# Weight blocks split once: pass 2 stores both parts in scratch memory, passes 3 and 4 fetch them

## The chip, the cores and the metric

The kernel runs on one core of a Trainium2 chip. The metric is the time of one execution on the device in microseconds (us), as the median of several runs. The engines are TensorE (PE, with its weight loads PEld), VectorE (DVE), ScalarE (ACT), GpSimd (POOL) and SyncE (SP), which here issues all DMA transfers, in one queue and in program order.

## The reference, cut to what matters

One layer of a decoder: an adaLN-modulated RMS norm, one input projection, a sliding-window attention branch (A) and a gated linear recurrence (B), each projected and merged by sigmoid gates, an output projection, and a gated residual. There are 2048 prompt positions (D_MODEL 1024) and 8 sample positions with caches of their own, all in float32.

```python
h = rms_norm(x, norm_g) * (1 + scale) + shift
proj = h @ w_in                      # qa, ka, va, za, qb, fb, ib, zb
ya = window_attention(qa, k_all, v_all, pos0, sinks) * silu(za)
o, s_new = hgrn2_chunked(qb, log_f, k_in, ib, s0)
yb = rms_norm(o, o_norm_g) * silu(zb)
g_a, g_b = split(sigmoid(h @ w_merge + b_merge), 2)
y = g_a * (ya @ w_proj_a) + g_b * (yb @ w_proj_b)
out = x + gate * (y @ w_out)
```

## The kernel before

The prompt is worked on in four passes (`it` 0 to 3, called pass 1 to 4) of 512 positions. A pass has 68 units of dense matmuls (`UNITS`): four each of B, A, za, f, qb, ib and zb, then 32 merge units (ga, gb, pa, pb), then four each of o0 and o1, the two halves of the output projection. The units alternate between two PSUM banks, D0 and D1. Each unit is done in two halves, and between the halves each engine runs the small tasks that `SIDE` lists for that place: transposes, attention, the recurrence, and in passes 1 and 2 the work for the sample rows.

The weights are 58 blocks (`BLOCKS`) of 128 x 1024 floats, 512 KB each, and every pass reads all of them again. To keep float32 precision, each factor is split into a high part in the matmul's reduced format and the low rest, and a product is three matmuls: high x high, high x low, low x high. A block comes by DMA into one of three raw buffers (`w_raw`). ACT copies it into the high part (`split_hi`, L969), POOL subtracts in four pieces to get the low part (`split_lo`, L1691). Both parts go into one of eight slots (`w_hi`, `w_lo`; `SLOT`), two of which the attention's output holds for part of a pass. `HOLDER[n]` is the unit that reads the slot's former block last, `SPOT[n]` the unit at which block n is split, planned so that the split is some 7 cost units (a unit of 24 matmuls counts 4) ahead of the first use. A unit waits for the semaphore w_lo of its last block.

SP's order is written out: `weights(n)` loads raw block n when block n - 3 is split and, in passes 1 and 2, when the sample rows have been multiplied with it in its raw form (the task `bu`, L807 to L814; two blocks at a time where `PAIR` says so). Other transfers (x tiles, stores of the result, caches, the sample's states) are events with a due unit, put into the same queue ahead of the first weight load that is due later. Among them, at the end of pass 1 and the start of pass 2, are the stores of the result rows, and the eight state loads `s_st` (L616), 256 KB each. POOL scales a state (L1751), DVE adds the product of PE's task `vB` (L1626), and PE uses it in the task `so` (L856).

Before the first pass PE transposes four tiles of x (`x_turn`, L704). Two are done ahead of the first unit, two are tasks inside it (L154, L155).

Of the kernel before, what the change touches and what calls it, by code (L numbers as in the profile page):

```python
# [15 lines left out]
TB, NIT = 512, 4  # L16
# [119 lines left out]
def put(it, u, hf, task, a, bank=None, key=None):  # L136

    SIDE.setdefault((it, u, hf), []).append((task, a, bank, key or (it, task, a)))
# [12 lines left out]
    put(it, n // 2, n % 2, *rest)  # L151


put(0, 0, 0, "xturn", 2)  # L154
put(0, 0, 1, "xturn", 3)  # L155
for it in range(NIT):
    if it == 0:
        put(0, 3, 0, "gm", 0, "XA")
# [88 lines left out]
for _it in range(NIT):  # L247
    for _u in UNITS:
        if _u in TH:
# [6 lines left out]
           "lvl", "dgp", "at0", "smax", "p_exp", "p_norm", "kst", "on", "yf", "yh", "yl", "y7f", "y7h", "y7l", "x_in0", "x_in1", "xst", "rstd",  # L256
           "xn", "xm", "xh0", "xh1", "h_hi", "h_lo", "grow", "s_rows", "s_th", "s_sq8", "s_sc", "s_exp", "s_p", "ckv", "s_oT",
           "s_f", "s_ib", "esel", "s_sq", "s_yb", "s_y", "s_o", "s_o1", "s_win", "s_st_out", "xsr"]
        + ["vr"] + [f"xr{t}" for t in range(NT)] + [f"out{t}" for t in range(NT)] + [f"s_st{b}" for b in range(NS)]
        + [f"ada{k}" for k in range(2 * KT)] + [f"gw{p}" for p in range(4)]  # L260
        + ["p_late", "p_load0", "p_load1", "p_load2", "p_load3", "p_load4", "p_c", "p_T", "p_xs", "p_mod", "hm", "p_vec", "p_lb", "p_exp0", "p_rows", "p_scale", "p_x2",
           "p_x3", "p_bg", "fin", "w_lo0", "act_step", "dve_step", "pool_step"])


def h_pairs(it, n):
# [54 lines left out]
def build(nc, A, O):  # L320

    ctx = ExitStack()
    with ctx:
# [95 lines left out]
        def f32(ap):  # L419
            return ap.bitcast(F32)  # L420
# [34 lines left out]
        XA, XB, XC, XD = (pb[b] for b in ("XA", "XB", "XC", "XD"))  # L455
        S = {n: ctx.enter_context(nc.semaphore("s_" + n)) for n in SEMS}

        def flat(t, n):
            return t.rearrange("p h n -> p (h n)")[:, 0:n]

# [15 lines left out]
            return [(w_raw[:, n % NRAW], A["w_blocks"][n % NB].rearrange("p (k c) -> p k c", k=KT))]  # L476

        came, _c = [], [0] * NRAW
        for n in range(NIT * NB):
            _c[n % NRAW] += 16 * len(block_dmas(n))  # L480
            came.append(_c[n % NRAW])
        bursts, bursts_so_far = {}, 0
# [15 lines left out]
        def _(sp):  # L498
# [21 lines left out]
            for k in range(KT):  # L520
                ada_load(k, 0)

            def weights(n):
                if n >= NRAW:
                    s.wait_ge("w_lo", n - NRAW + 1)
                    if n - NRAW in bursts:
                        s.wait_ge(*bursts[n - NRAW])
                for dst, src in block_dmas(n):
                    load(dst, src, f"w_in{n % NRAW}")
# [116 lines left out]
            load(sink_s[:, :], A["sinks"].rearrange("a h -> h a"), "p_load4", allow_slow_non_contiguous=True)  # L646
            s.full(-1, "xT", 1)
            load(bg, A["b_ada"][:, 2 * D:3 * D].broadcast_to([P, D]), "p_bg")
            for n in range(NRAW, NIT * NB):
                while events and events[0][0] <= max(SPOT[n - NRAW], BURST_AT.get(n - NRAW, 0)):  # L650
                    event(*events.pop(0)[1])
                weights(n)
            for _, e in events:
                event(*e)
            s.wait_ge("k_sc", NIT)
# [12 lines left out]
        def _(pe):  # L668
# [18 lines left out]
            def turn_rows(h):  # L687
                bank, c = ((pb["D0"], 0), (XC, P))[h]
                for i in range(8):
                    n = 4 * h + i % 4 + 8 * (i // 4)  # L690
                    ins = mm(bank[:, c + 9 * i:c + 9 * i + 9], mod_rows[:, P * n:P * n + P], sel, start=True, stop=True)
                s.done(ins, "p_T")
# [21 lines left out]
            ada_half(1)  # L714
            s.wait_ge("p_rows", 4)
            turn_rows(1)

            def dense(it, u, hf_):
                kind, j = UNITS[u]
                blocks = unit_blocks(u)  # L720
                bank = pb[f"D{u % 2}"]
                s0, nb = SLOT[blocks[0]], len(blocks)
                if hf_ == 0:
                    s.wait_ge(f"D{u % 2}_free", (it * NU + u) // 2)
                    s.wait_ge("w_lo", it * NB + blocks[-1] + 1)
                    if (kind, j) == ("pa", 0):
                        s.wait_ge("yl", 16 * it + 4)
                    if (kind, j) == ("pb", 0):
                        s.wait_ge("yl", 16 * it + 8)
                hi, lo, k0, nk = h_hi, h_lo, 0, KT  # L730
                if kind == "pa":
                    hi, lo, nk = ya_hi, ya_lo, 4
                elif kind == "pb":
                    hi, lo, k0, nk = yb_hi, yb_lo, 4, 4
                elif kind in OUT_COLS:
                    hi, lo = y_hi, y_lo
                if it == 0 and u < NT:
                    s.wait_ge("h_lo", (1, 3, 2, 4, 5, 6, 7, 8)[2 * u + hf_])
                for k in range(hf_ * nk // 2, (hf_ + 1) * nk // 2):
                    if it and u == 0:  # L740
                        s.wait_ge("h_lo", h_pairs(it - 1, k // 2))
                    if u == 60:
                        s.wait_ge(*(("yl", 16 * it + 9 + k) if k < 7 else ("y7l", it + 1)))
                    if u == 61:
                        s.wait_ge("yl", 16 * it + 16)
                    for r, (w, a) in enumerate(((w_hi, hi), (w_hi, lo), (w_lo, hi))):
                        go, end = (k == 0 and r == 0), (k == nk - 1 and r == 2)
                        if kind in ("A", "B", "ib", *OUT_COLS):
                            ins = mm(bank[:, 0:P * nb].rearrange("p (n c) -> p n c", c=P), a[:, k, P * j:P * j + P],  # L749
                                     w[:, s0:s0 + nb, k, :], start=go, stop=end)  # L750
                        else:
                            ins = mm(bank[:, :], w[:, s0, k0 + k, :], a[:, k, :], start=go, stop=end)  # L752
                if hf_:
                    s.done(ins, f"D{u % 2}_full")
# [206 lines left out]
        def _(act):  # L961
# [3 lines left out]
            def split_hi(n):  # L965
                s.wait_ge(f"w_in{n % NRAW}", came[n])
                if HOLDER[n] >= 0:
                    s.unit_full(*divmod(HOLDER[n], NU))
                s.done(fn(w_hi[:, SLOT[n % NB]], w_raw[:, n % NRAW], ACT.Copy), "w_hi")  # L969

            def squares(src, t, junk):
# [163 lines left out]
            for it in range(NIT):  # L1135
                for u in range(NU):
                    for hf_ in (0, 1):
                        if hf_:
                            evac(it, u)
                            if UNITS[u] == ("pb", 7):  # L1140
                                s.wait_ge("y7f", it + 1)
                                s.done(fn(y_hi[:, 7, 0:P], yf[:, 1, 0:P], ACT.Copy), "y7h")
                                s.wait_ge("yf", 8 * it + 8)
                                s.done(fn(y_hi[:, 7, P:TB], yf[:, 1, P:TB], ACT.Copy), "yh", 16 * it + 16)
                            for n in ATTACH.get(it * NU + u, []):
                                split_hi(n)
                        for task, a, _, key in SIDE.get((it, u, hf_), []):
                            side(it, task, a, key)
                            if task == "PV":
                                s.freed(it, "PV", a)  # L1150
                                if it == 1 and a == 0:
                                    s.wait_ge("s_st_out", 16 * NS)
                                high(ya_hi[:, :, P * a:P * a + P], 16 * it + a)
                            if task == "PV" and a == 3:
                                s.done(fn(kT[:, 0:P], kT[:, TB:TB + P], ACT.Copy))
                                s.full(it, "PV", 3)
                                s.done(fn(vtok[:, 0, :], vtok[:, NT, :], ACT.Copy))
                            if task == "yT":
                                s.freed(it, "yT", a)
                                high(yb_hi[:, :, P * a:P * a + P], 16 * it + 4 + a)  # L1160
                        if hf_ and UNITS[u][0] == "pb" and UNITS[u][1] < 7:
                            j = UNITS[u][1]
                            s.wait_ge("yf", 8 * it + j + 1)
                            high(y_hi[:, j, :], 16 * it + 8 + j)
# [518 lines left out]
        def _(pool):  # L1683
# [34 lines left out]
            for it in range(NIT):  # L1718
                for u in range(NU):
                    for hf_ in (0, 1):  # L1720
                        if hf_:
                            if UNITS[u] == ("pb", 7):
                                s.wait_ge("y7h", it + 1)
                                s.done(g_.tensor_tensor(y_lo[:, 7, 0:P], yf[:, 1, 0:P], f32(y_hi[:, 7, 0:P]), ALU.subtract), "y7l")
                                s.wait_ge("yh", 16 * it + 16)
                                s.done(g_.tensor_tensor(y_lo[:, 7, P:TB], yf[:, 1, P:TB], f32(y_hi[:, 7, P:TB]),
                                                        ALU.subtract), "yl", 16 * it + 16)
                            for n in ATTACH.get(it * NU + u, []):
                                split_lo(n)
                        for task, a, _, key in SIDE.get((it, u, hf_), []):  # L1730
                            if task == "at0":
                                if it:
# [105 lines left out]
```

## Time and profile before

| | |
|---|---|
| Median of 3 runs | 1563.0 us (1561.78 to 1563.56) |
| The profiled execution | 1561.99 us, its span 1559.9 us |
| Mean granted TensorE clock | 0.998 |
| PE, ACT, DVE, POOL busy | 98%, 35%, 51%, 53% of the span |
| Bytes moved by DMA | 178.94 MB, 115 GB/s on average |

The span runs from the first to the last instruction. Busy times of different engines overlap. A matmul's end is modelled, so a busy PE is not a PE at its peak. The chain of waits follows the work that ended last back to its start. A wait is put down to the instruction that released it. The granted clock is 1.0 at 2.4 GHz and 0.5 at 1.2 GHz.

### The profile page before, as it was taken

Reading aid. Unit: us, or ns where it says so; the run is one execution under the profiler, and the core shown is the slowest. Engines: PE = TensorE matmul, PEld = TensorE weight load, DVE = VectorE, ACT = ScalarE, POOL = GpSimd, SP = SyncE. Lnnn points to the kernel's source line nnn. Section 1 sums busy time; section 2 is a strip of 40 time slices with the busy share of each in tenths; the row PEclk is TensorE's granted clock in tenths of the full one; section 3 lists DMA queues with packets and bytes.
Section 4 is the critical chain, followed back from the end, with each engine's and each line's share of the span. In section 5 each row is a group of like instructions: output and inputs, shape, how many; then the busy total and the mean of one; then the engine's idle time right before and its main releaser. Section 6 shows DMA issues by size and latency. Waiting matters only on the chain.

```text
span 1559.9 us, 31668 instructions
## 1 busy us (share of the span) xinstructions
PE 1529.6 (98%) x13056; PEld 1242.1 (80%) x13056; DVE 792.2 (51%) x1900; ACT 541.2 (35%) x1119; POOL 821.8 (53%) x1074
## 2 busy tenths in 40 slices
PE   5999999999999999999999999999999999999998
PEld 2777778877888778887779878888888877788887
DVE  5767464234578866231544774622453775623132
ACT  4334324344322532434331452243432353143330
POOL 1525434557863643365783472437886363437671
PEclk9999999999999999999999999999999999999999
DMA  9612211334464221233343331223543231222241
GB/s 343 237 55 83 83 57 55 114 130 162 163 197 114 103 69 61 77 109 109 136 175 124 102 110 42 83 70 113 207 155 145 75 109 56 75 72 92 103 167 59
DMA packets 62791, 178.94 MB, mean 115 GB/s; under 512 B 7087, under 2 KB 18696, under 8 KB 61865
## 3 DMA queue, kind: packets, MB, share of 16 engines
q1 hardware_dynamic: 62648, 176.93, 32.4%
q8 instruction: 103, 1.69, 0.4%
q14 instruction: 40, 0.32, 0.1%
HBM read 162.84 MB, written 11.96 MB: 112 GB/s over the span
## 4 chain that ended last, share of the span: by engine, by line
PE 94%; DVE 3%; SPq 1%; DMA 1%; issue 1%; ACT 0%; POOL 0%; DVEq 0%
PE ps_D L752 56%; PE ps_D L749 25%; PE ps_XD L814 2%; PE ps_XA L912 1%; SPq L502 1%; PE ps_XB L890 1%; PE ps_XB L938 1%; PE ps_XA L943 1%; PE ps_XB L937 1%; PE ps_XA L923 1%; PE ps_XA L890 1%; DMA th_t<-in_w_ada 1%; PE ps_XB L923 1%; PE ps_XC L825 0%; PE ps_XC L930 0%
## 5 line engine op out<-in xcount | busy, mean ns | idle before, releaser
L1691 POOL TENSOR_TENSOR w_lo_t<-w_raw,w_hi_t 128x256 fp32r<-128x256 f32 x920 | 677.0, 770 | 604.6 <-ACT w_hi_t L969 604.1
L752 PE MATMUL ps_D<-h_hi_t,w_hi_t 128*128 128x512 f32 x1024 | 412.2, 403 | 0.0
L752 PE MATMUL ps_D<-h_lo_t,w_hi_t 128*128 128x512 f32 x1024 | 399.7, 390 | 0.0
L752 PE MATMUL ps_D<-h_hi_t,w_lo_t 128*128 128x512 f32 x1024 | 399.6, 390 | 0.0
L969 ACT ACTIVATE w_hi_t<-w_raw 128x1024 fp32r<-128x1024 f32 x232 | 240.0, 1051 | 121.7 <-PE ps_D L749 61.6
L752 PEld LDWEIGHTS ps_D<-h_hi_t,w_hi_t 128*128 128x128 f32 x1024 | 192.3, 188 | 47.2 <-issue 10.1
L752 PEld LDWEIGHTS ps_D<-h_hi_t,w_lo_t 128*128 128x128 f32 x1024 | 192.2, 188 | 41.8
L752 PEld LDWEIGHTS ps_D<-h_lo_t,w_hi_t 128*128 128x128 f32 x1024 | 192.5, 188 | 36.2
L749 PE MATMUL ps_D<-w_hi_t,h_hi_t 128*128 128x384 f32 (+1 forms) x384 | 141.7, 369 | 4.1 <-POOL w_lo_t L1691 3.1
L749 PE MATMUL ps_D<-w_hi_t,h_lo_t 128*128 128x384 f32 (+1 forms) x384 | 136.6, 356 | 0.0
L749 PE MATMUL ps_D<-w_lo_t,h_hi_t 128*128 128x384 f32 (+1 forms) x384 | 136.4, 355 | 0.0
L749 PE MATMUL ps_D<-w_hi_t,y_hi_t 128*128 128x512 f32 x256 | 100.2, 391 | 1.5 <-issue 1.5
L749 PE MATMUL ps_D<-w_lo_t,y_hi_t 128*128 128x512 f32 x256 | 99.7, 389 | 0.0
L749 PE MATMUL ps_D<-w_hi_t,y_lo_t 128*128 128x512 f32 x256 | 99.6, 389 | 0.0
L749 PEld LDWEIGHTS ps_D<-w_hi_t,h_hi_t 128*128 128x128 f32 x384 | 72.7, 189 | 15.0 <-issue 4.9
L1365 DVE SCALAR_TENSOR_TENSOR acc_t<-th_t,ps_D 128x512 f32<-128x512 f32 x24 | 16.5, 688 | 130.9 <-PE ps_D L752 130.8
L1036 ACT ACTIVATE th_t<-ps_D,bm_half 128x512 f32<-128x512 f32 x48 | 33.1, 689 | 139.2 <-PE ps_D L752 139.2
L1112 ACT ACTIVATE p_or_hf<-p_or_hf,sm 128x160 f32<-128x160 f32 x128 | 53.4, 419 | 77.5 <-DVE sm L1492 74.3
L749 PEld LDWEIGHTS ps_D<-w_lo_t,h_hi_t 128*128 128x128 f32 x384 | 72.6, 189 | 5.3
L749 PEld LDWEIGHTS ps_D<-w_hi_t,h_lo_t 128*128 128x128 f32 x384 | 72.8, 190 | 4.7
L1445 DVE TENSOR_TENSOR qq<-qq,ff 128x1024 f32<-128x1024 f32 x28 | 40.7, 1452 | 69.3 <-PE ps_XB L890 44.8
L1534 DVE SCALAR_TENSOR_TENSOR state<-state,ff,ps_XA 128x128 f32<-128x128 f32 x64 | 18.0, 342 | 112.4 <-PE ps_XA L943 112.4
(399 smaller groups left out, 2338.3 us busy)
## 6 DMA issues: line engine op xcount, KB each, us to landing
w_raw<-in_w_blocks SPq DMA_DIRECT2D x232, 512.0 KB, 3.3
xr<-in_x_prompt SPq DMA_DIRECT2D x16, 512.0 KB, 5.6
x_or_AT<-in_x_prompt SPq DMA_DIRECT2D x14, 512.0 KB, 4.5
out_dram<-xr SPq DMA_DIRECT2D x12, 512.0 KB, 2.9
x_or_AT<-in_x_turned SPq DMA_DIRECT2D x3, 1024.0 KB, 6.8
p_or_hf<-in_x_turned SPq DMA_DIRECT2D x3, 1024.0 KB, 7.4
out_dram<-xr SPq DMA_DIRECT2D x8, 256.0 KB, 2.0
ibtok<-vtok SPq DMA_DIRECT2D x8, 192.0 KB, 2.9
```

The source lines that it names most:

```text
L749: ins = mm(bank[:, 0:P * nb].rearrange("p (n c) -> p n c", c=P), a[:, k, P * j:P * j + P], w[:, s0:s0 + nb, k, :], start=go, stop=end)
L752: ins = mm(bank[:, :], w[:, s0, k0 + k, :], a[:, k, :], start=go, stop=end)
L814: ins = mm(dst, hS[:, k, :], raw[:, :, k, :], start=k < 4, stop=k >= 4)
L890: ins = mm(bank[row:row + left, m * col:m * col + m], kk[:, h, c + 32 * g:c + 32 * g + left], right, start=True, stop=True)
L923: ins = mm(dst[DH * g:DH * g + DH], val[:, DH * g:DH * g + DH], PT[r, g, :, 32 * j:32 * j + 32], start=j == 0, stop=j == 4)
L969: s.done(fn(w_hi[:, SLOT[n % NB]], w_raw[:, n % NRAW], ACT.Copy), "w_hi")
L1036: s.leave(fn(dst, bank[:, :], ACT.Tanh, scale=0.5, bias=bm_half[:, c:c + 1]), it, u)
L1112: fn(p_t[:, m, :], p_t[:, m, :], ACT.Exp, bias=negm[:, m:m + 1], accum_out=rsum[:, m:m + 1])
L1365: leave(stt(acc[:, :], thx("ga", j), 1.0, bank[:, :], ALU.add, ALU.mult), it, u)
L1445: s.done(tt(qr, qr, fl[:, :, :, 0:1].broadcast_to(shape), ALU.mult))
L1534: ins = stt(state[:, h, :], state[:, h, :], ff[:, h, P * a:P * a + 1], bank[:, P * h:P * h + P], ALU.mult, ALU.add)
L1691: ins = g_.tensor_tensor(w_lo[:, c, k:k + 2], w_raw[:, n % NRAW, k:k + 2], f32(w_hi[:, c, k:k + 2]), ALU.subtract)
```

## The change

In pass 2 the blocks are loaded and split as before, and SP then also stores both parts of each block into a scratch tensor in device memory (`kept`). In passes 3 and 4 raw loads and splits are gone: SP fetches both parts of a block from the scratch tensor straight into the slot, as soon as the slot's former block has been read for the last time. PE waits for the slot's fetches (`w_got`) there instead of for w_lo. A split into a slot waits until the slot's stores have landed (`w_kept`). Apart from that, one transposition of x is moved from inside the first unit to just ahead of it.

```diff
-put(0, 0, 0, "xturn", 2)
-put(0, 0, 1, "xturn", 3)
+put(0, 0, 0, "xturn", 3)
...
+def slot_loads(n):
+
+    return sum(SLOT[m % NB] == SLOT[n % NB] for m in range(2 * NB, n + 1))
+
+
+def slot_stores(n):
+
+    return sum(SLOT[m % NB] == SLOT[n % NB] for m in range(NB, min(n, 2 * NB)))
...
+        kept = nc.dram_tensor("w_kept", [NB, 2, P, KT * P], F32, kind="Internal").ap()
...
-        for n in range(NIT * NB):
+        for n in range(2 * NB):
             _c[n % NRAW] += 16 * len(block_dmas(n))
...
+            def keep(n):
+                if n >= NB:
+                    c = SLOT[n % NB]
+                    for h, w in enumerate((w_hi, w_lo)):
+                        load(kept[n % NB, h], f32(w[:, c]).rearrange("p k c -> p (k c)"), f"w_kept{c}")
+
+            def fetch(n):
+                c = SLOT[n % NB]
+                s.unit_full(*divmod(HOLDER[n], NU))
+                s.wait_ge(f"w_kept{c}", 32 * slot_stores(n))
+                for h, w in enumerate((w_hi, w_lo)):
+                    load(f32(w[:, c]).rearrange("p k c -> p (k c)"), kept[n % NB, h], f"w_got{c}")
+
             def weights(n):
                 if n >= NRAW:
                     s.wait_ge("w_lo", n - NRAW + 1)
+                    keep(n - NRAW)
                     if n - NRAW in bursts:
                         s.wait_ge(*bursts[n - NRAW])
...
-            for n in range(NRAW, NIT * NB):
+            for n in range(NRAW, 2 * NB):
                 while events and events[0][0] <= max(SPOT[n - NRAW], BURST_AT.get(n - NRAW, 0)):
                     event(*events.pop(0)[1])
                 weights(n)
+            for n in range(2 * NB - NRAW, 2 * NB):
+                while events and events[0][0] <= max(SPOT[n], BURST_AT.get(n, 0)):
+                    event(*events.pop(0)[1])
+                s.wait_ge("w_lo", n + 1)
+                keep(n)
+            for n in range(2 * NB, NIT * NB):
+                while events and events[0][0] <= HOLDER[n]:
+                    event(*events.pop(0)[1])
+                fetch(n)
...
+            x_turn(-1, 2, x_p[2])
...
-                    s.wait_ge("w_lo", it * NB + blocks[-1] + 1)
+                    if it < 2:
+                        s.wait_ge("w_lo", it * NB + blocks[-1] + 1)
+                    else:
+                        for b in blocks:
+                            s.wait_ge(f"w_got{SLOT[b]}", 32 * slot_loads(it * NB + b))
...
+                s.wait_ge(f"w_kept{SLOT[n % NB]}", 32 * slot_stores(n))
                 s.done(fn(w_hi[:, SLOT[n % NB]], w_raw[:, n % NRAW], ACT.Copy), "w_hi")
...
                             for n in ATTACH.get(it * NU + u, []):
-                                split_hi(n)
+                                if n < 2 * NB:
+                                    split_hi(n)
...
+                                if it == 2 and a == 0:
+                                    for c in (NSLOT, NSLOT + 1):
+                                        s.wait_ge(f"w_kept{c}", 32)
...
                             for n in ATTACH.get(it * NU + u, []):
-                                split_lo(n)
+                                if n < 2 * NB:
+                                    split_lo(n)
```

## Rows read from the trace of the kernel before

**Rows 1.** The page: engines' busy time, and two costliest groups of the split.

```profile
PE 1529.6 (98%) x13056; PEld 1242.1 (80%) x13056; DVE 792.2 (51%) x1900; ACT 541.2 (35%) x1119; POOL 821.8 (53%) x1074
...
L1691 POOL TENSOR_TENSOR w_lo_t<-w_raw,w_hi_t 128x256 fp32r<-128x256 f32 x920 | 677.0, 770 | 604.6 <-ACT w_hi_t L969 604.1
...
L969 ACT ACTIVATE w_hi_t<-w_raw 128x1024 fp32r<-128x1024 f32 x232 | 240.0, 1051 | 121.7 <-PE ps_D L749 61.6
```

**Rows 2.** Windows: passes 2, 3, 4; length, busy PE, PEld, DVE, ACT, POOL.

```profile
450.08:834.94 384.86, 381.94 (x3303) 309.06 (x3301) 209.18 (x497) 132.76 (x272) 214.68 (x277) 1.00 0.34 116
834.94:1194.92 359.98, 359.45 (x3037) 300.28 (x3036) 182.16 (x421) 129.46 (x266) 206.43 (x269) 1.00 0.32 111
1194.92:1554.25 359.33, 358.77 (x3029) 299.18 (x3027) 162.53 (x388) 116.10 (x242) 180.11 (x237) 1.00 0.26 90
```

**Rows 3.** Waits of PE, 834.94 to 1554: us in total, times, longest.

```profile
PE ps_XA L890 <- issue: 1.1, 2, 0.6
```

**Rows 4.** Chain of waits, two long pieces: start us, us, what.

```profile
1060.84 65.34 PE ps_D L752 x288
...
1420.91 89.82 PE ps_D L752 x396
```

**Rows 5.** The page's DMA issues: KB each, median us from issue to landing.

```profile
w_raw<-in_w_blocks SPq DMA_DIRECT2D x232, 512.0 KB, 3.3
...
out_dram<-xr SPq DMA_DIRECT2D x12, 512.0 KB, 2.9
```

**Rows 6.** Windows as in rows 2; last three columns: clock, DMA share, GB/s.

```profile
40.00:43.60 3.60, 3.29 (x10) 3.30 (x11) 1.69 (x6) 0.95 (x2) 2.81 (x3) 0.50 1.02 420
442.00:452.00 10.00, 10.00 (x48) 8.60 (x47) 4.01 (x7) 1.06 (x1) 0.52 (x1) 1.00 0.88 315
```

**Rows 7.** Timelines of ACT and PE, end of pass 3: start us, us, what.

```profile
1140.72 0.69 ACT L1036 ACTIVATE th_t<-ps_D,bm_half 128x512 f32<-128x512 f32 x1 [3.80 <-PE ps_D L752]
...
1151.40 0.39 PE L749 MATMUL ps_D<-w_hi_t,y_hi_t 128*128 128x512 f32 x1
```

**Rows 8.** Timeline of SP, pass 1 into pass 2.

```profile
441.65 0.34 SPq L502 DMA_DIRECT2D out_dram<-xr  x1
...
451.79 0.34 SPq L502 DMA_DIRECT2D out_dram<-xr  x1
452.18 2.59 SPq L502 DMA_DIRECT2D s_st_hi<-in_state_hgrn  x4
```

**Rows 9.** The tile s_st_hi, 452.1 to 452.6: the first state load.

```profile
DMA to landing us min/median/max: 3.4/3.4/3.4
```

**Rows 10.** Timeline of POOL, DVE and PE, 458.5 to 462.

```profile
458.84 1.05 POOL L1751 TENSOR_TENSOR s_st_hi<-s_st_hi,smS 128x512 f32<-128x512 f32 x1
...
460.37 1.12 DVE L1626 SCALAR_TENSOR_TENSOR s_st_hi<-ps_XD,smS,s_st_hi 128x128 f32<-128x128 f32 x4
...
461.60 0.43 PE L856 MATMUL ps_XC<-s_st_hi,p_or_hf 128*32 128x128 f32 x8 [0.17 <-issue]
```

**Rows 11.** Timeline, 784 to 797, end of pass 2.

```profile
784.59 1.76 SPq L502 DMA_DIRECT2D xr<-in_x_prompt  x4
...
787.03 0.47 PE L749 MATMUL ps_D<-w_hi_t,y_hi_t 128*128 128x512 f32 x1 [1.47 <-issue]
...
794.81 1.06 ACT L969 ACTIVATE w_hi_t<-w_raw 128x1024 fp32r<-128x1024 f32 x1 [6.48 <-DMA w_raw<-in_w_blocks]
...
795.90 1.07 PE L814 MATMUL ps_XD<-w_raw,hS_or_yS 128*32 128x256 f32 x16
```

**Rows 12.** Timeline, 38 to 45, start of the first unit.

```profile
38.29 1.37 DVE L1242 TENSOR_SCALAR p_or_hf<-ps_XA,gscale,shift 128x128 f32<-128x128 f32 x4
...
40.30 0.69 PE L749 MATMUL ps_D<-w_hi_t,h_hi_t 128*128 128x384 f32 x1 [3.11 <-POOL w_lo_t L1691]
...
44.10 1.04 PE L704 MATMUL ps_XA<-ident,s_st_lo 128*128 128x128 f32 x8
```

More of the change, by code:

```diff
@@ L258 @@
            "s_f", "s_ib", "esel", "s_sq", "s_yb", "s_y", "s_o", "s_o1", "s_win", "s_st_out", "xsr"]
-        + ["vr"] + [f"xr{t}" for t in range(NT)] + [f"out{t}" for t in range(NT)] + [f"s_st{b}" for b in range(NS)]
+        + ["vr"] + [f"w_got{c}" for c in range(NSLOT + 2)] + [f"w_kept{c}" for c in range(NSLOT + 2)] + [f"xr{t}" for t in range(NT)] + [f"out{t}" for t in range(NT)] + [f"s_st{b}" for b in range(NS)]
         + [f"ada{k}" for k in range(2 * KT)] + [f"gw{p}" for p in range(4)]
```

## The prediction

> **What bounds the kernel now.** I read the page's engine shares first. TensorE is busy 98% of the span, the split of the weights is the costliest group on POOL (920 subtractions, 677 us) and one of the largest on ACT (232 copies, 240 us), and both engines are far from full [rows 1]. Then the windows by pass, because this change touches pass 2 in one way and passes 3 and 4 in the other. Pass 2 (450.08 to 834.94) has 384.86 us with PE busy for 381.94; pass 3 has 359.98 with 359.45; pass 4 has 359.33 with 358.77 [rows 2]. So in the two passes that lose their splitting, PE stands still for about 0.5 us each, and the list of its waits there names neither the split nor a transfer: 1.1 us in two waits on the recurrence [rows 3]. The chain of waits gives the spacing of the 512-column matmuls: 65.34 us over 288 in pass 3 and 89.82 over 396 in pass 4, 0.227 us each [rows 4]. It does not move with how busy DMA or POOL is in the two passes (111 and 90 GB/s, POOL 206 and 180 us) [rows 2, 4]. PE is the bound of passes 3 and 4 and runs at a fixed step there; an emptier ACT and POOL cannot shorten it.
>
> **What it removes.** In passes 3 and 4, 116 copies of 1.05 us (122 us of ACT) and 464 subtractions of 0.77 us (357 us of POOL) [rows 1]. Gain on the path: at most the PE idle time of the two passes, 0.5 + 0.6 = 1.1 us; its releaser is not the split, so I take 0 (bounds 0 and -1.1).
>
> **What it adds in passes 3 and 4.** 232 fetches of 512 KB in place of 116 raw loads. One load takes 3.3 us from issue to landing [rows 5], and a second half megabyte behind it 1.25 us more (at 420 GB/s, a stretch with DMA's share at its full value [rows 6]), so a pair lands 4.6 us after its issue. A fetch cannot start before the slot's last reader is through, which raw loads could. The shortest cover that I find is out3, whose slot is held by gb7: its unit is done when ACT starts its tanh at 1140.72, and the first output unit starts at 1151.40 [rows 7]; 10.7 - 4.6 leaves 6 us. q1 and q2 come behind the last store of the pass before, and out5 to out7 behind 2 MB of x; by the same prices I find 6.5 and 7 us there. PE's new waits (w_got, up to four ahead of a unit) would stop everything behind them on PE, but they find their semaphores set. Cost 0; if one fetch came 7 us later than this, it would cost about 1 us in each of two passes.
>
> **What it adds in pass 2.** 116 stores of 512 KB, issued by SP as soon as a block is split, each pair ahead of the next raw load in the same queue. A lone store lands in 2.9 us [rows 5] and SP spends 0.34 us to issue one [rows 8]: SP waits most of its time, so the issues are free. The bytes are not: a raw load lands 2.5 us later than before, by 420 GB/s. Most blocks have some 10 us between the split and the unit that uses it, and ACT's added wait (split_hi now also waits for the slot's store, issued tens of us earlier) hides too. What is queued behind a late split on ACT is the next tanh or copy out of a bank, which has a unit (5.4 us) to spare. Two places have no such cover.
>
> First, the eight state loads. SP issues three x stores and three raw loads from 441.65 on, one more store at 451.79, and the first state load at 452.18 [rows 8]; it lands 3.4 us later, at 455.6 [rows 9]. Its reader on POOL starts at 458.84, after a split, and takes 1.05; DVE follows at 460.37, and PE reads the result at 461.60 after a wait of 0.17 [rows 10]. PE has no slack there. With the change three pairs of stores (blocks k0, v0, q0) enter that queue: 13 half megabytes up to the last x store instead of 7. The first lands at 441.65 + 2.9 = 444.5; twelve more and the first 256 KB state load follow. At 420 GB/s (1.25 us each, 0.6 for the last) that ends at 460.1. But the stretch 442 to 452, with stores and loads mixed, moved 315 GB/s at a share of 0.88 [rows 6], which is 358 at a full share: 1.46 us each, 0.7 for the last, 462.8. I take the middle, 461.4, being unable to tell the two. POOL then ends at 462.45 instead of 459.89, DVE starts at 462.5 instead of 460.37: +2.1 us on PE (bounds 0.9 and 3.5, and 0 if the queue drains better than both).
>
> Second, the end of pass 2. PE multiplies the sample's rows with the raw blocks out4 and out5 at 795.90 [rows 11] and needs out5's raw load, which landed just before ACT's copy at 794.81, behind four x tiles issued at 784.59 [rows 11]. Now out2's two stores stand between those tiles and out5's load: 794.8 + 2.5 = 797.3, PE waits 1.4 us (by 358 GB/s 1.8; 0 if the transfers overlap). A few us before, the first output unit starts at 787.03 after a wait of 1.47 for out3's split [rows 11]; out3's raw load is issued ahead of the new stores, so that wait stays and isn't counted again. Sum for pass 2: 2.1 + 1.4 = 3.5 us.
>
> **What it moves.** The third transposition of x goes ahead of the first unit. It needs bank XA, freed at 38.29 + 1.37 = 39.7, while the first unit starts at 40.30, after 3.11 us of waiting for a split [rows 12]. Eight transposes took 1.04 us at the upper clock [rows 12]; at 40 the granted clock is 0.5, so 2.1 us by that row. 0.6 of it falls in the wait, 1.5 pushes the first unit back, and 1.04 disappears after it: +0.5. PE works 0.6 us earlier, and if the clock rises earlier by as much, 0.3 comes back. If the clock stayed up, the low clock's cost would go too: ten matmuls in 3.29 us [rows 6] at 0.32 instead of the later 0.175, some 1.5 us, plus 0.6. I take 0 (bounds -2.1 and +0.6).
>
> **The Trainium skill.** On DMA the skill speaks against the change more than the fast row does: its page DMA: Bandwidth & Descriptors, section Where 436 GB/s comes from, says that for transfers between HBM and SBUF the HBM side, about 358 GB/s, binds. The trace exceeds that with loads alone (420) and matches it in the mixed stretch (315 at 0.88). By that figure alone the sum for pass 2 would be 5.3.
>
> **Sum.** The profiled execution took 1561.99 us (span 1559.9). 1561.99 + 0 + 3.5 + 0 = 1565.5. The median of the three runs, 1563.0, lies 1.0 above this execution, so I forecast 1566.5. A measurement of this kernel can tell 0.2%, 3.1 us, from no change: 1559.9 to 1566.1. The forecast lies on that bound, its own range is 1564.5 to 1568.
>
> **Rivals.** Forecast: pass 2 loses at two places, nothing is won: 1566.5, chance 0.42.
>
> Hidden: the stores drain beside the loads, or reach the queue in its pauses (the share was 0.88, not 1), and neither place waits more than now: 1563.0 less up to 1 at the start, 1562 to 1564. For it speaks that pass 2 moves only 116 GB/s on average [rows 2]. Against it, both places sit in bursts. Chance 0.26.
>
> The HBM bound: all mixed stretches run at 358, as the stretch 442 to 452 would: 3.5 + 1.8 = 5.3, 1568.3. This is the skill's rule of above. Chance 0.15.
>
> Slower by a queue that lengthens itself: the x tiles and out5, 2.5 MB after 784.59, needed until 794.8 [rows 11], some 260 GB/s. At that pace a half megabyte takes 2.0 us, the state load comes at 469.5 (444.5 + 12 x 2.0 + 1.0) and PE waits 10 us; at out5 it waits 794.8 + 4.0 - 795.9 = 2.9. 1563.0 + 13 = 1576. It decides from the point where the two lates together pass 3.1 us. Against it: seven transfers did go at 315 in just that stretch. Chance 0.12.
>
> Faster: the clock stays up at the start (-2.1), both recurrence waits go (-1.1), nothing is late: 1559.8. Chance 0.05; there is nothing else on PE to win.
>
> **Chances and range.** Slower by over 0.2%: 0.26 of the forecast's 0.42, the 0.15 and the 0.12: 0.53. Within: 0.16 + 0.24 of the hidden case + 0.02 of the faster one: 0.42. Faster: 0.05. The range 1561 to 1575 leaves out the faster case, the edge of the hidden one and half of the slowest.
>
> **What would show it.** After: passes 3 and 4 still near 360 us, POOL in them emptier by about 180 us each, no PE wait on the slots' fetches. In pass 2, PE waiting some 2 us for the state products near 462 and over 1 us for raw blocks near 796, and pass 2 near 388. The first unit at about 41.8, if the clock is low there. The prediction is wrong if a fetch shows among PE's waits, if pass 2 is no longer than 385, or if PE's 0.227 us step changes under the larger traffic.

## The result, and the profile after

The changed kernel takes 1567.1 us (median of 8, 1566.07 to 1568.99), the kernel before 1562.3 (8 runs, 1561.78 to 1563.56): a ratio of 1.0031, 95% interval 1.0022 to 1.004. The profiled execution took 1567.19, its span is 1565.4, 5.5 more than before.

Windows of the three passes after the change, columns as in [rows 2] (clock, DMA share and GB/s last):

```profile
449.51:838.72 389.21, 382.47 (x3303) 309.19 (x3301) 205.35 (x497) 129.16 (x268) 204.04 (x265) 1.00 0.72 264
838.72:1199.61 360.89, 359.54 (x3038) 300.30 (x3037) 155.75 (x421) 74.19 (x208) 35.49 (x37) 1.00 0.53 195
1199.61:1559.78 360.17, 359.04 (x3029) 299.08 (x3027) 139.80 (x388) 64.72 (x188) 20.81 (x17) 1.00 0.47 173
```

Against [rows 2], pass 2 is 4.35 us longer and passes 3 and 4 are 0.9 and 0.8 longer, although POOL has lost 171 and 159 us in them. The two long pieces of the chain, which answer to [rows 4], say that PE's step is what it was (65.34 over 288, 89.82 over 396):

```profile
1065.52 65.34 PE ps_D L791 x288
...
1426.44 89.82 PE ps_D L791 x396
```

So the time went into stops of PE. Before the change its list of waits in pass 2 has one over 0.5 us, at the first output unit [rows 11]:

```profile
PE ps_D L749 <- issue: 1.5, 1, 1.5
```

Its waits after the change, in pass 2 and then in passes 3 and 4:

```profile
PE ps_XD L853 <- DMA w_raw<-in_w_blocks: 2.0, 1, 2.0
PE ps_D L788 <- issue: 1.9, 1, 1.9
PE ps_XA L951 <- DVE yf_t L1572: 0.7, 1, 0.7
...
PE ps_XC L895 <- issue: 0.4, 1, 0.4
PE ps_XD L847 <- DMA w_raw<-in_w_blocks: 0.3, 1, 0.3
```

```profile
PE ps_XA L929 <- issue: 1.3, 1, 1.3
PE ps_D L791 <- issue: 0.8, 1, 0.8
PE ps_D L788 <- issue: 0.3, 1, 0.3
```

To see what each is worth, match PE's instructions of the two traces one by one and note where the second falls further behind. Behind the start of pass 1 it is 0.6 us ahead. Then it loses 0.2 at the state product (461), 0.9 at the attention scores (545), 0.8 at two places near 757 to 760, 0.5 at the first output unit (789), 2.0 at the raw block out5 (800), 0.9 in pass 3 (nearly all at 987) and 0.8 in pass 4 (mostly at 1314). That is the 5.5.

**Out5**, the place predicted. PE and ACT wait for the raw load, issued at 788.66 behind four x tiles and out2's two stores, as the rows of SP, PE and ACT show:

```profile
785.89 1.76 SPq L513 DMA_DIRECT2D xr<-in_x_prompt  x4
787.70 0.43 SPq L513 DMA_DIRECT2D w_kept<-w_hi_t  x1
788.17 0.44 SPq L513 DMA_DIRECT2D w_kept<-w_lo_t  x1
788.66 0.66 SPq L513 DMA_DIRECT2D w_raw<-in_w_blocks  x1
...
799.72 1.07 PE L853 MATMUL ps_XD<-w_raw,hS_or_yS 128*32 128x256 f32 x16 [1.97 <-DMA w_raw<-in_w_blocks]
...
799.70 1.06 ACT L1009 ACTIVATE w_hi_t<-w_raw 128x1024 fp32r<-128x1024 f32 x1 [9.58 <-DMA w_raw<-in_w_blocks]
```

**The attention scores**, a place not predicted. Read the rows of ACT, DVE and PE from the top: a split waits 3.85 us for its raw load, the exponentials of the softmax stand behind it on ACT, DVE waits 2.55 for their sum, PE 0.69 for DVE. Before the change (the first two rows) the same split was one of two done from 534.17 on, and the exponentials started at 538.48.

```profile
534.17 2.00 ACT L969 ACTIVATE w_hi_t<-w_raw 128x1024 fp32r<-128x1024 f32 x2
538.48 0.43 ACT L1112 ACTIVATE p_or_hf<-p_or_hf,sm 128x160 f32<-128x160 f32 x1 [2.31 <-DVE sm L1492]
```

```profile
539.56 1.06 ACT L1009 ACTIVATE w_hi_t<-w_raw 128x1024 fp32r<-128x1024 f32 x1 [3.85 <-DMA w_raw<-in_w_blocks]
540.52 0.41 ACT L1152 ACTIVATE p_or_hf<-p_or_hf,sm 128x160 f32<-128x160 f32 x1
...
542.46 0.37 DVE L1551 TENSOR_TENSOR sm<-sm 128x4 f32<-128x4 f32 x1 [2.55 <-ACT sm L1153]
...
544.77 0.51 PE L951 MATMUL ps_XA<-kT,qT_or_szb 64*32 64x160 f32 x16 [0.69 <-DVE yf_t L1572]
```

**The states** were not late: POOL came to the first at 458.23, it had landed at 456.30 (451.60 + 4.7), and PE's wait is 0.36 where it was 0.17 [rows 10]. These answer to [rows 8 to 10]:

```profile
435.49 0.34 SPq L513 DMA_DIRECT2D out_dram<-xr  x1
...
451.60 0.43 SPq L513 DMA_DIRECT2D s_st_hi<-in_state_hgrn  x1
...
458.23 1.05 POOL L1796 TENSOR_TENSOR s_st_hi<-s_st_hi,smS 128x512 f32<-128x512 f32 x1
...
461.21 0.42 PE L895 MATMUL ps_XC<-s_st_hi,p_or_hf 128*32 128x128 f32 x8 [0.36 <-issue]
```

The first x store left at 435.49, not 441.65 [rows 8]. It waits for a DVE addition that had taken 6.87 us before the change, beside 16 subtractions of POOL without a pause, and took 1.28 now, in the middle of 12 such subtractions. DVE's addition and POOL's subtractions before, then the addition after:

```profile
434.75 6.87 DVE L1385 TENSOR_TENSOR xr<-xr,acc_t 128x512 f32<-128x512 f32 x1
...
429.72 11.36 POOL L1691 TENSOR_TENSOR w_lo_t<-w_raw,w_hi_t 128x256 fp32r<-128x256 f32 x16 [0.25 <-ACT w_hi_t L969]
```

```profile
434.18 1.28 DVE L1429 TENSOR_TENSOR xr<-xr,acc_t 128x512 f32<-128x512 f32 x1
```

The long addition ended at 441.62, 0.55 us after the last subtraction of POOL's row (441.07). The other long ones of the profiled executions (6.87 in e12, 4.09 in e2, and 5.36 for an earlier addition in e7) also ended 0.55 us after such a row. So the long additions got on only when POOL's row was through. The change did not decide it: e3 has the 16 subtractions without a pause and took 1.28, and e6 and e12, which are the same program up to pass 3, took 1.27 and 6.87.

**Passes 3 and 4.** PE stops inside a burst of 128 small matmuls of the recurrence, with nothing named that it waits for:

```profile
984.27 1.12 PE L929 MATMUL ps_XA<-qq,kk 128*32 128x16 f32 x110
986.74 0.36 PE L929 MATMUL ps_XA<-qq,kk 128*32 128x16 f32 x18 [1.35 <-issue]
```

The page's DMA queues name a second one, q8, for instructions: 103 packets of 16 KB, which keep step with PE's 26,112 matmuls and weight loads, so I take them for PE's own instruction loads. What speaks for it: in the 14 profiled kernels PE has 35 stops of over 0.2 us in passes 3 and 4, and every one ends 1.2 to 1.6 us after the end of such a packet. One such packet starts at 984.49, while four block fetches (4 MB), issued from 981.65 on, fill the engines. The DMA queues from 984.4 to 984.6 (packets, MB, share of 16 engines):

```profile
q1 hardware_dynamic: 22, 0.08, 101.0%
q8 instruction: 1, 0.02, 29.6%
```

It took 0.95, and PE went on 1.3 us after its end. In pass 4 the stop comes behind the small matmuls of the attention's fourth product (from 1310.72), with a packet from 1312.22. Before the change the packet for this place started 0.95 us ahead of the burst (979.49, burst 980.44), now 0.22 behind its start. The Trainium skill (Runtime: NRT & Kernel Launch, section Instruction fetch mechanics) says that instructions come in blocks of 16 KiB through a DMA queue of the engine's own, a crossing being mostly hidden: the size agrees (16,384 bytes a packet), the hiding holds for most of the 103 packets and not for these.

### The profile page after: what moved, and what is told of

Its sections match the earlier page's. It is cut to its first block, busy times and chain, and to the rows that moved or that the text cites. A ratio compares the mean times of both kernels' runs of the same rounds, so it can differ in the third digit from the quotient of the medians.

```text
span 1565.4 us, 31357 instructions
## 1 busy us (share of the span) xinstructions
PE 1530.5 (98%) x13056; PEld 1242.2 (79%) x13056; DVE 734.4 (47%) x1900; ACT 431.0 (28%) x1003; POOL 481.7 (31%) x610
## 4 chain that ended last, share of the span: by engine, by line
PE 90%; DVE 3%; DMA 3%; SPq 2%; POOL 1%; issue 1%; ACT 1%; DVEq 0%; ACTq 0%
PE ps_D L791 53%; PE ps_D L788 24%; DMA w_raw<-in_w_blocks 3%; SPq L513 2%; PE ps_XD L853 1%; PE ps_XA L951 1%; PE ps_XB L929 1%; POOL w_lo_t L1735 1%; PE ps_XB L977 1%; PE ps_XA L982 1%; PE ps_XB L976 1%; PE ps_XA L929 1%; PE ps_XA L962 1%; PE ps_XC L969 0%; PE ps_XB L962 0%
## 5 line engine op out<-in xcount | busy, mean ns | idle before, releaser
L1735 POOL TENSOR_TENSOR w_lo_t<-w_raw,w_hi_t 128x256 fp32r<-128x256 f32 x456 | 336.5, 772 | 330.5 <-ACT w_hi_t L1009 330.5
L1009 ACT ACTIVATE w_hi_t<-w_raw 128x1024 fp32r<-128x1024 f32 x116 | 120.6, 1052 | 82.6 <-DMA w_raw<-in_w_blocks 60.3
L1751 POOL TENSOR_TENSOR w_lo_t<-yf_t,w_hi_t 128x512 fp32r<-128x512 f32 x16 | 20.8, 1301 | 281.1 <-ACT w_hi_t L1098 281.1
L1751 POOL TENSOR_TENSOR yb_lo_t<-yf_t,yb_hi_t 128x512 fp32r<-128x512 f32 x16 | 20.5, 1288 | 218.6 <-ACT yb_hi_t L1098 218.6
L1751 POOL TENSOR_TENSOR y_lo_t<-yf_t,y_hi_t 128x512 fp32r<-128x512 f32 x28 | 36.2, 1292 | 151.2 <-ACT y_hi_t L1098 150.7
```

The costliest lines, as they stand in the source:

```text
L1735: ins = g_.tensor_tensor(w_lo[:, c, k:k + 2], w_raw[:, n % NRAW, k:k + 2], f32(w_hi[:, c, k:k + 2]), ALU.subtract)
L1751: s.done(g_.tensor_tensor(dst, src, f32(hi), ALU.subtract), "yl", n + 1)
```

## The experiments

All of them in one table: lengths of the passes and the span from the profiled execution, the median of all executions, its ratio to the kernel before on the same chip.

| kernel | pass 2 | pass 3 | pass 4 | span | median | ratio (95%) |
|---|---|---|---|---|---|---|
| before | 384.86 | 359.98 | 359.33 | 1559.9 | 1562.3 | |
| changed | 389.21 | 360.89 | 360.17 | 1565.4 | 1567.1 | 1.0031 (1.0022 to 1.004) |
| e1 loads first | 387.19 | 362.69 | 360.14 | 1564.4 | 1566.0 | 1.0021 (1.0012 to 1.0029) |
| e2 stores only | 389.39 | 359.70 | 359.00 | 1564.9 | 1566.6 | 1.0027 (1.0017 to 1.0038) |
| e3 fetches only | 385.06 | 361.13 | 359.86 | 1561.6 | 1563.0 | 1.0005 (0.9996 to 1.0014) |
| e4 x turn back | 389.51 | 361.12 | 359.96 | 1567.8 | 1569.0 | 1.0041 (1.0028 to 1.0055) |
| e5 fetches held | 388.85 | 360.01 | 360.16 | 1564.5 | 1566.3 | 1.0031 (1.0017 to 1.0045) |
| e6 all mended | 385.19 | 359.77 | 359.93 | 1559.6 | 1561.8 | 1.0006 (0.9995 to 1.0016) |
| e7 one pair more | 393.45 | 360.83 | 360.40 | 1569.9 | 1571.9 | 1.0063 (1.005 to 1.0075) |
| e8 x turn only | 385.25 | 359.72 | 359.57 | 1559.9 | 1562.1 | 0.9997 (0.9989 to 1.0006) |
| e9 ib1 held | 385.27 | 360.01 | 360.29 | 1561.7 | 1561.5 | 0.999 (0.9982 to 0.9999) |
| e10 out earlier | 388.31 | 359.52 | 360.25 | 1563.0 | 1564.2 | 1.0007 (0.9998 to 1.0016) |
| e11 states behind more | 393.64 | 362.73 | 359.87 | 1570.8 | 1572.6 (one) | |
| e12 zb0 held | 390.13 | 359.45 | 359.24 | 1563.8 | 1561.3 | 0.9995 (0.9986 to 1.0004) |

**The two halves of the change apart.** e2 stores in pass 2 and goes on loading and splitting in passes 3 and 4 (PE waits for w_lo there, ACT and POOL split every block, as before):

```diff
             def keep(n):
-                if n >= NB:
+                if NB <= n < 2 * NB:
...
-            for n in range(NRAW, 2 * NB):
+            for n in range(NRAW, NIT * NB):
...
-            for n in range(2 * NB, NIT * NB):
-                fetch(n)
```

> The changed kernel with pass 2 storing every block as there, but with passes 3 and 4 loading raw blocks and splitting them on ACT and POOL as before the change (nothing is fetched back). Theory: the stores alone make pass 2 as long as in the changed kernel (389.2), and without the fetches passes 3 and 4 return from 360.9 and 360.2 to 360.0 and 359.3, since there the doubled traffic makes PE's own instruction loads late: about 1565.3 us. Rival: the 0.9 us of each of the passes 3 and 4 are not the fetches' doing (chance of one execution, or a stall that any order of PE's instructions has): passes 3 and 4 stay near 360.9 and 360.2, the time at 1567. A rival for pass 2, that its length comes from this one execution: pass 2 other than 388.5 to 390.

e3 stores one block alone and fetches it for all:

```diff
             def keep(n):
-                if n >= NB:
+                if n == ONLY:
...
-                    load(f32(w[:, c]).rearrange("p k c -> p (k c)"), kept[n % NB, h], f"w_got{c}")
+                    load(f32(w[:, c]).rearrange("p k c -> p (k c)"), kept[0, h], f"w_got{c}")
```

> Leaves out the stores of all blocks but one; in passes 3 and 4 the parts of this one block are fetched in the place of every block's. So no store burdens pass 2, and passes 3 and 4 have the changed kernel's fetches and no splits. Theory: pass 2 returns to 384.9 to 385.3, passes 3 and 4 stay at about 360.9 and 360.2 (the fetches' price, and an emptied ACT and POOL bring nothing), the time is 1562.5 to 1563. Rival: the relief of ACT and POOL is worth something that the stores hide: passes 3 and 4 below 360.0 and 359.3, the time below 1561. Second rival, the fetches cost nothing: passes 3 and 4 at 360.0 and 359.3, the time 1561.

The stores own pass 2's loss (389.39 against 385.06), the fetches own that of passes 3 and 4 (721.0 together with them, 718.7 without; 721.1 in the changed kernel, 719.3 before). An emptied ACT and POOL bring nothing that shows: e3's passes 3 and 4 are not shorter than before, and e12 below, which has the fetches without their two stops, takes 718.7 as e2 does. e2's median came out 1.3 above the sum; its profiled execution reached the state product later than the changed kernel's by 1.85 us, by its start for the most part.

**Order or bandwidth?** e1 puts a block's stores behind the next raw load.

```diff
                     s.wait_ge("w_lo", n - NRAW + 1)
-                    keep(n - NRAW)
...
                 for dst, src in block_dmas(n):
                     load(dst, src, f"w_in{n % NRAW}")
+                if n >= NRAW:
+                    keep(n - NRAW)
```

> The two stores of a block are issued just behind the next raw load instead of just ahead of it; bytes and everything else as in the changed kernel (pass 2 there 389.2 us, before the change 384.9). Theory, order in the queue: what pass 2 loses is raw loads that land some 2.4 us later because 1 MB of stores stands ahead of them. Then the 2.0 us wait of the sample rows for block out5 near 800 goes, so do the 0.7 us near 545 and most of 0.9 us near 757 to 760 and 0.5 near 789, and pass 2 comes to 385 to 386 us, the time to about 1563.5. Rival, bandwidth: the stores cost the same wherever they stand, since they share the 16 DMA engines with the loads: pass 2 stays at 388 to 389 and the time at 1566.5 to 1567.

PE's waits in pass 2 of e1:

```profile
PE ps_D L789 <- issue: 2.0, 1, 2.0
PE ps_XC L896 <- DVE s_st_lo L1671: 0.5, 1, 0.5
PE ps_XC L896 <- DVE s_st_hi L1671: 0.4, 1, 0.4
PE ps_XA L963 <- DVE sm L1538: 0.4, 1, 0.4
PE ps_XC L896 <- issue: 0.4, 1, 0.4
```

The waits of 545, 757 to 760 and 800 are gone, with the same bytes: it was the order. The pass is still 1.6 above the expected 385.6, because the wait that was left, 2.0 us at the first output unit, was followed by a low clock (windows, clock third from the end), and so was the stop in pass 3:

```profile
786.40:790.50 4.10, 4.07 (x11) 3.23 (x12) 2.39 (x4) 1.33 (x2) 4.10 (x6) 0.58 1.03 415
...
984.00:988.60 4.60, 4.43 (x29) 3.55 (x30) 3.19 (x5) 0.00 (x0) 0.00 (x0) 0.63 1.02 409
```

Matched with before, PE loses 1.6 us to the clock in each. That is more than what was missing from the expected 1563.5 (the profiled execution took 1566.2).

e7 measures the price of the bytes, by a second pair of stores at one place:

```diff
+TWICE = NB + BIX[("out", 2)]
...
+                    if n == TWICE:
+                        for h, w in enumerate((w_hi, w_lo)):
+                            load(kept[NB, h], f32(w[:, c]).rearrange("p k c -> p (k c)"), f"w_kept{c}")
```

> The changed kernel with the stores of one block, out2, done twice (into a second place), so that 2 MB instead of 1 MB of stores stand between the four x tiles and out5's raw load. Theory: out5's load lands later by 1 MB at the full rate of some 410 GB/s, 2.5 us: PE's wait for it near 800 goes from 2.0 to 4.4 us, all other waits stay, pass 2 comes to 391.7, the time to 1569.5. Rival: that wait has another cause (a late split, ACT's order): it stays at 2.0 and pass 2 at 389.2.

```profile
PE ps_XD L859 <- DMA w_raw<-in_w_blocks: 4.4, 1, 4.4
```

The wait is 4.4 as expected, 2.4 us for 1 MB. The pass is another 1.7 longer than that, by a low clock behind the wait:

```profile
802.60:806.00 3.40, 3.40 (x20) 1.92 (x17) 0.00 (x0) 0.91 (x1) 2.41 (x4) 0.50 1.03 420
```

**The states.** e11 does the same for k0 and v0 (`TWICE = (NB + 1, NB + 2)`):

> The changed kernel with the stores of the two blocks k0 and v0 done twice: 2 MB more ahead of the state loads. In the changed kernel the first state landed at 456.30, and POOL came to it only at 458.23: 1.9 us to spare, so PE's wait for the product near 461 was 0.36. Theory: 2 MB at 410 GB/s make the states 5 us later, 461.2; POOL then waits for them, ends at 462.3, DVE takes 1.1, PE waits 2.6 us near 463.5. Rival: the queue ahead of the states has pauses that take up the bytes: PE's wait there stays below 1 us.

The first state landed at 461.09 and PE waited 3.3 us at 463.56. From landing to PE it is 2.47 us (POOL 1.05, DVE 1.13, the rest between them). So in the changed kernel's profiled execution there was slack, up to a landing of about 458.7, and the step's price was right. e12, below, met the condition that this execution missed.

**The stops in passes 3 and 4.** e5 holds some fetches back:

```diff
             def fetch(n):
                 c = SLOT[n % NB]
                 s.unit_full(*divmod(HOLDER[n], NU))
+                if n % NB == BIX[("ib", 2)]:
+                    s.full(n // NB, "PV", 2)
+                if n % NB in (BIX[("zb", 2)], BIX[("zb", 3)], BIX[("ga", 0)], BIX[("gb", 0)]):
+                    s.full(n // NB, "level", 3)
```

> The changed kernel, but in passes 3 and 4 five fetches are issued later: ib2's behind the attention's third product, and zb2, zb3, ga0, gb0 (4 MB that the changed kernel issues at once when the last ib unit ends, 981.65 in pass 3) behind the next small matmuls of the recurrence. All have units to spare. Theory: PE's own instruction loads queue behind the fetches' packets; the one that starts at 984.49 (1.2 us later in PE's stream than before the change) makes PE stand still for 1.35 us at 986.7, the one at 1312.22 for 0.83 at 1314.6. With the fetches held back both loads come in time: pass 3 goes from 360.9 to 360.1, pass 4 from 360.2 to 359.5, the time from 1567.1 to about 1565.6. Rival: PE's stream alone (a burst of 256 small instructions needs two loads within 2 us) makes the stops, whatever else moves: both stay as they are and the time at 1567.

In pass 3 it did what it should (the instruction packet starts 1.23 ahead of the burst, the stop is 0.52, the pass 360.0). In pass 4 the stop stayed at 0.69: I had held the wrong fetch. The median, 1566.3 (1564.2 to 1573.9), is 0.7 above the expected. e9, which puts the three mends of e6 together with ib1 held as well, repeats the mistake:

> As the run with all three mends, with ib1's fetch held back behind the attention's third product too. There pass 4 kept a stop of 0.49 us at 1308.6: PE's instruction load started at 1306.25, in the tail of ib1's fetch (issued 1302.45, landed 1306.91). Theory, queueing: with this fetch later the load starts earlier and the stop goes; pass 4 from 359.9 to 359.4, the time 1561.3. Rival, PE's stream: the stop stays near 0.5.

There the stop was 0.83. (e9's ratio is the only one whose interval lies below 1, at 0.9982 to 0.9999; among so many comparisons that shows no gain.) The fetch in flight is zb0's, and e12 holds that:

```diff
+                if n % NB == BIX[("zb", 0)]:
+                    s.full(n // NB, "PV", 3)
```

> As the run with all three mends, but with zb0's fetch held back behind the attention's fourth product instead of ib2's behind the third. The two runs that held ib1 and ib2 held the wrong fetch: the attention's fourth product starts 2.6 us after the fetch of zb0 was issued (1310.72 and 1308.11 in the changed kernel), and in the runs so far PE's instruction load there starts later, and PE stands still longer, the later that fetch is in flight. Theory, queueing: with zb0 held the stop near 1309 (0.49 to 0.83 us) goes, pass 4 takes 359.4 to 359.6, the time is 1561 or a little less. Rival, PE's stream: the stop stays at 0.5 or more, pass 4 at 359.9 to 360.3.

Pass 4 of e12 takes 359.2, and one wait is left of PE's in passes 3 and 4:

```profile
PE ps_D L799 <- issue: 0.4, 1, 0.4
```

Over all runs, with the packet's start and end counted from the start of the burst of small matmuls (us, from the traces):

| | packet's start | packet's end | PE's stop |
|---|---|---|---|
| pass 3, no fetches (before, e2, e8) | -0.96 to -0.92 | -0.04 to +0.34 | 0.24 to 0.53 |
| pass 3, fetches in flight (changed, e1, e3, e4, e7, e11) | +0.22 to +0.46 | +1.17 to +1.42 | 1.34 to 1.62 |
| pass 3, fetches held (e5, e6, e9, e10, e12) | -1.23 to -0.64 | -0.29 to +0.32 | 0 to 0.52 |
| pass 4, no fetches (before, e2, e8) | +1.08 to +1.18 | +2.02 to +2.35 | none |
| pass 4, zb0's fetch in flight (changed, e1, e3 to e7, e9 to e11) | +1.17 to +1.61 | +2.07 to +2.49 | 0.49 to 1.01 |
| pass 4, zb0's fetch held (e12) | +0.08 | +1.00 | none |

So the fetches make PE's instruction packets late. In pass 3 the stop goes with the packet's end: ends of -0.29 and -0.18 left none, -0.06 to +0.04 about 0.25, +0.21 to +0.34 about 0.52. In pass 4 the kernels without fetches have ends like those with, and no stop. In pass 3 their stop falls ahead of the burst's 113th matmul, in all kernels with fetches that stop there ahead of the 111th, so a packet does not hold the same instructions in both; whether that is the reason was not tested.

**All mends.** e6 is e1, e5 and late stores for the output blocks:

```diff
+LATE = NB + BIX[("out", 0)]
...
-                    keep(n - NRAW)
...
                 for dst, src in block_dmas(n):
                     load(dst, src, f"w_in{n % NRAW}")
+                if n >= NRAW and n - NRAW < LATE:
+                    keep(n - NRAW)
...
+                if n == 2 * NB - NRAW:
+                    for m in range(LATE, n):
+                        keep(m)
```

> Three mends together: stores behind the next raw load (as in the run with loads first), the fetches held back (as in the run with held fetches), and the eight output blocks stored only when the last raw block has been split, near 803. Theory: no raw load is late any more; PE waits near 545, 758 and 800 are gone, the wait at the first output unit is back to 1.5 us, pass 2 takes 385.0, pass 3 360.1, pass 4 359.5, the time is 1561 to 1563, that of the kernel before. Rival, the clock: PE's waits of over 1.5 us are followed by 3.4 us at half the clock as in the run with loads first, at 1.6 us each: up to 1565.5. Second rival, the eight late stores and the first fetches of pass 3 collide, and a fetch shows among PE's waits near 835 to 845.

It came out as the theory has it, 385.2, 359.8 and 359.9, and 1561.8 us, no slower than before and not measurably faster. The rival's low clock was not in its profiled execution; two of its 12 executions took 1568.7.

e12's profiled execution shows how the rest varies. DVE's addition took 6.87 us again, and then the states came late (timeline of DVE, POOL and PE, and a window):

```profile
434.05 6.87 DVE L1440 TENSOR_TENSOR xr<-xr,acc_t 128x512 f32<-128x512 f32 x1
...
461.72 1.05 POOL L1807 TENSOR_TENSOR s_st_hi<-s_st_hi,smS 128x512 f32<-128x512 f32 x1 [3.58 <-DMA s_st_hi<-in_state_hgrn]
...
464.13 0.66 PE L906 MATMUL ps_XC<-s_st_hi,p_or_hf 128*32 128x128 f32 x8 [3.41 <-issue]
```

```profile
463.20:470.20 7.00, 6.07 (x24) 5.28 (x25) 6.10 (x19) 0.52 (x2) 4.47 (x7) 0.51 1.01 351
```

The first x store left at 440.94, the state landed at 461.65, PE waited 3.4 us, and from 463.3 to 470.2 the granted clock was 0.5; this execution took 1565.6. Three of its 12 took 1565.6 to 1566.2, the others 1559.2 to 1561.7. That the other two had the same cause fits, but only one was profiled.

**The moved transposition.** e4 undoes it, e8 makes it alone, in the kernel before.

```diff
-put(0, 0, 0, "xturn", 3)
+put(0, 0, 0, "xturn", 2)
+put(0, 0, 1, "xturn", 3)
...
-            x_turn(-1, 2, x_p[2])
```

> The changed kernel with the third transposition of x put back inside the first unit. Theory: the move gained 0.6 us (eight transposes at the low clock run in a wait of 2.9 us that PE had anyway): the first unit starts at 40.3 as before, and everything behind it is 0.6 us later, the time 1567.7. Rival: the move does nothing by itself, the 0.6 us came from a setup that was 0.3 us quicker in that execution and from the clock: the time stays at 1567.1 and unit 5 starts as early as in the changed kernel.

> The kernel before with the third transposition of x moved ahead of the first unit, and nothing else. Theory: the move by itself is worth the 1 to 2 us by which the changed kernel with the move undone was slower: 1560.5 to 1561.3 us, the fifth unit of pass 1 about 1 us earlier than before. Rival: the difference came from where the half clock of the start happened to end in those executions: 1562.3, the same as before.

e4 is 1.9 slower than the changed kernel, by intervals that overlap; e8 cannot be told from the kernel before. The move is worth between nothing and 2 us.

**A miss.** e10 tried to take away the wait of 1.5 us at the first output unit [rows 11], on top of e9:

```diff
-OUT_AT = (56.5, 57.5, 58, 59.5, 60.5, 61, 61.5, 62.5)
+OUT_AT = (56, 57, 58, 59.5, 60.5, 61, 61.5, 62.5)
```

> As the run just described, with the sample rows multiplied with out0 and out1 half a unit earlier in pass 2 (56 and 57 instead of 56.5 and 57.5), which frees a raw buffer for out3 some 2.7 us earlier. Theory: PE's wait at the first output unit, 1.5 us before the change and 1.6 with the mends, comes from that raw load and goes: pass 2 at 383.6, the time 1560 or a little less, below the kernel before. Rival: the wait ends on something else (the split's place on ACT, the gates ahead of it) and stays above 1 us, the time 1561.5.

The wait became 0.16, and the next one, 3.3 us on, 2.37, with a low clock behind it. out3's split had moved ahead of y's split on ACT and stood there 8.25 us, waiting for its raw load.

## Why the prediction came out, step by step

**PE is the bound, the relief is worth 0:** right. The step of 0.227 is unchanged under 195 GB/s, and e12, with ACT and POOL emptied, takes as long in passes 3 and 4 as e2, which splits every block (718.7 both). The two waits of [rows 3], read as waits on the recurrence, were stops of the other kind: each ended 1.3 us after the end of a packet of instructions.

**The fetches cost 0:** right for the slots, no fetch is among PE's waits. Wrong for the sum, by 1.7 us: I looked for who waits for the fetches and not for what else goes through the same DMA engines. PE's instruction packets do (e5, e12).

**States, +2.1:** measured 0.2. The count was right, 13 half megabytes from the first x store to the last. What failed is that I took the first store's start, 441.65, as given; it hung on a DVE addition beside POOL, 6.87 us there and 1.28 here. In e12's execution, with 6.87 again, the state landed at 461.65 (predicted 461.4) and PE reached the product at 464.13 (predicted 463.7), followed by a low clock that the sum did not have. The step is right for one kind of execution and not for the other.

**Out5, +1.4:** the place and mechanism right, 2.0 measured, outside the 0 to 1.8 that I gave it. The price of 2.5 us a pair is right (2.4 in e7). Mis-sized was the landing: 13.8 us after the first of the four x tiles was issued, not 10.2 + 2.5 = 12.7. I had counted out2's stores alone; out1's, issued at 780.59, held up out4's load, which was still under way when the tiles were issued (it landed at 788.08; before the change at 783.78, ahead of the tiles). PE came 0.5 us later to the place, which hid part of it.

**Other places of pass 2, 0:** wrong, and the step that failed in its reasoning: "what is queued behind a late split on ACT is the next tanh or copy out of a bank". At 540 it is the softmax (0.9 us). Near 757, the loads of two turned halves of x (2 MB) and four pairs of stores wait in one queue, and raw loads take 11 us (0.8). The wait for out3, of which I wrote that it stays, grew by 0.5: its load took 4.12 us instead of 3.59 with stores issued right behind it (3.68 in e6, which issues them later).

**The move, 0:** cannot be told from 0 (e4, e8).

**Rivals.** Hidden: no at out5, which waited 2.0; at the states nearly so, by the early x store. Self-lengthening queue: no, out5 waited 2.0 and not 2.9, the states cost 0.2. The 358 GB/s of the Trainium skill (DMA: Bandwidth & Descriptors, section Where 436 GB/s comes from) did not bind the stretch with stores and loads mixed:

```profile
442.00:452.00 10.00, 10.00 (x49) 8.68 (x48) 3.54 (x5) 1.06 (x1) 1.61 (x3) 1.00 1.03 410
```

Over the whole 10 us it moved more. Nor is 410 a fixed rate: e12's window above moved 351 at a full share.

The sum of 3.5 met 5.5 in the spans of the profiled executions and 4.8 in the medians, the forecast of 1566.5 the measured 1567.1. That it came so near was in good part luck. Of the 5.5 only 2.2 came from the two places that I had named; the 1.9 too much at the states made up for part of what I had left out. And the median of three that the forecast starts from, 1563.0, was 0.7 above that of eight, 1562.3.

## What to carry to other kernels

A store costs the loads that share its queue: here a pair made the load behind it 2.4 us later, and the load just ahead of it 0.5 us longer. Issue it behind the next load and, where loads are short of time, later still. Hold a large burst of transfers until the engine has passed its bursts of small instructions. For every load that becomes later, go down the waiting engine's own order to what stands behind, in every place where it happens and not only where the slack looks smallest. A duration that came from two engines in each other's way is no fixed number: find out how else it can come out before a start time is built on it.

## What the runs showed of the hardware

PE's instructions come in packets of 16 KB through the DMA engines that move the data; with four block fetches (4 MB) issued just ahead, the packet for a burst started 0.22 to 0.46 us behind the burst's start, 1.2 us ahead of it in four of the five kernels that held the fetches back. PE stood still for 1.34 to 1.62 us with the late packet, for 0 to 0.52 with the early one, and went on 1.2 to 1.6 us after the end of the packet.

The same DVE addition of two 128x512 tiles beside POOL's subtractions took 0.9 to 1.3 us in eleven of the profiled executions, 4.09 in one and 6.87 in two. The long ones ended 0.55 us after POOL's unbroken row of subtractions did. What decides between the two is open.

With some waits of PE the granted clock fell to 0.5 (1.2 GHz): with those of 3.26, 3.41 and 4.39 us, and with some between 1.6 and 2.4 (e1, e10, e11), while others of that length (1.95 and 1.97 in the changed kernel, 2.28 in e4) were followed by none. A fall that lasted 3.4 us cost PE some 1.6 us (e1).
